# A two-block transformer kernel: maxima from one product over 128 rows, row copies two slots behind TensorE, and the up projections' high and low activations in one product of 512 columns

## The reference

```
m_inter = b + m;  m_t = max(m_inter, max_s d_log)           # running maxima of the mLSTM
w_intra = exp(d_log - m_t);  s = (q k^T) * w_intra          # 8 heads, forward and backward
...
y = concat(m_lat, d_lat) @ w_out
x = x + ga1 * rmsnorm(y, g_post_mix)
h = modulate(rmsnorm(x, g_pre_ffn), sh2, sc2)
u = dwconv3(h @ w_up, conv_w, conv_b)                       # w_up: 2048 x 11264
gate, val = split(u)
x = x + ga2 * rmsnorm((silu(gate) * val) @ w_down, g_post_ffn)
```

## Time and profile before

| | |
|---|---|
| median of 3 runs | 3097.32 us (3096.26 to 3098.8) |
| the profiled execution | 3095.88 us, its span 3093.8 us |
| TensorE busy | 2956.6 us, 96% |
| VectorE, ScalarE, GpSimd busy | 2098.6, 1498.0, 143.8 us |
| mean granted clock | 0.983 |
| HBM | 203 GB/s over the span |

### The profile page before, as it was taken

One profiled execution on the slowest core, in us unless ns is written; L12 is line 12 of the kernel. 1 busy time (PEld: TensorE's weight loads), 2 busy tenths in 40 slices (PEclk: granted clock), 3 DMA queues, 4 the chain that ended last, 5 costly groups with the idle time before them and its releaser, 6 DMA issues.

```text
span 3093.8 us, 44809 instructions
## 1 busy us (share of the span) xinstructions
PE 2956.6 (96%) x17608; PEld 2555.2 (83%) x17608; DVE 2098.6 (68%) x2514; ACT 1498.0 (48%) x1935; POOL 143.8 (5%) x109
## 2 busy tenths in 40 slices
PE   7799999998799999999999889999999999999998
PEld 2478888985679989998997768999987888888876
DVE  6888766557465654665566898754555555899987
ACT  6722222446455544453444423744444444777775
POOL 0000000000000000000000466000000000000000
PEclk9899999999999999999999989999999999999999
DMA  9768777530155555555554334455545655999996
GB/s 373 254 219 297 272 262 244 184 117 28 48 171 163 177 190 190 179 187 190 184 183 150 123 109 150 154 183 188 177 144 164 187 179 176 310 343 347 340 349 240
DMA packets 425402, 628.70 MB, mean 203 GB/s; under 512 B 13168, under 2 KB 234368, under 8 KB 424864
## 3 DMA queue, kind: packets, MB, share of 16 engines
q1 hardware_dynamic: 423504, 615.57, 60.1%
q0 software_dynamic: 1744, 10.98, 0.9%
HBM read 624.40 MB, written 2.10 MB: 203 GB/s over the span
## 4 chain that ended last, share of the span: by engine, by line
PE 86%; DVE 9%; issue 2%; ACT 2%; DMA 1%; POOL 1%; SPq 0%; DVEq 0%; ACTq 0%; POOLq 0%
PE acc L2422 12%; PE acc L2380 11%; PE acc L2419 11%; PE acc L2420 11%; PE acc L2381 11%; PE acc L2383 11%; PE acc L2400 2%; PE acc L2401 2%; PE acc L2403 2%; DVE w_lo L386 1%; DVE w_lo L383 1%; PE acc L2808 1%; PE acc L2806 1%; PE acc L2805 1%; PE acc L2875 1%
## 5 line engine op out<-in xcount | busy, mean ns | idle before, releaser
L368 ACT ACTIVATE w_hi<-w_raw 128x1024 fp32r<-128x1024 f32 x521 | 552.0, 1059 | 771.4 <-PE acc L2383 286.6
L383 DVE TENSOR_TENSOR w_lo<-w_raw,w_hi 128x1024 fp32r<-128x1024 f32 x521 | 641.2, 1231 | 385.7 <-ACT w_hi L368 382.7
L386 DVE TENSOR_TENSOR w_lo<-w_raw,w_hi 128x1024 fp32r<-128x1024 f32 x521 | 649.7, 1247 | 353.3 <-ACT w_hi L370 350.7
L370 ACT ACTIVATE w_hi<-w_raw 128x1024 fp32r<-128x1024 f32 x521 | 549.7, 1055 | 536.8 <-PE acc L2383 303.9
L2380 PE MATMUL acc<-h_pair,w_hi 128*128 128x256 f32 x2368 | 592.8, 287 | 14.6 <-ACT w_hi L368 10.4
L2381 PE MATMUL acc<-h_pair,w_hi 128*128 128x256 f32 x2368 | 589.2, 286 | 0.0
L2380 PEld LDWEIGHTS acc<-h_pair,w_hi 128*128 128x128 f32 x2368 | 461.3, 195 | 23.7 <-issue 23.6
L2381 PEld LDWEIGHTS acc<-h_pair,w_hi 128*128 128x128 f32 x2368 | 461.6, 195 | 0.2
L2419 PE MATMUL acc<-w_hi,h_pair 128*128 128x512 f32 x896 | 354.6, 396 | 14.6 <-ACT w_hi L368 14.3
L2383 PE MATMUL acc<-h_pair,w_lo 128*128 128x256 f32 x2368 | 335.5, 285 | 19.9 <-DVE w_lo L383 19.9
L2420 PE MATMUL acc<-w_hi,h_pair 128*128 128x512 f32 x896 | 350.6, 391 | 0.0
(11 more groups left out here) (501 smaller groups left out, 3663.8 us busy)
## 6 DMA issues: line engine op xcount, KB each, us to landing
w_raw<-in_w_in SPq DMA_DIRECT2D x116, 1024.0 KB, 5.2
w_raw<-in_w_mod SPq DMA_DIRECT2D x96, 1024.0 KB, 5.4
w_raw<-in_w_up SPq DMA_DIRECT2D x176, 512.0 KB, 4.3
w_raw<-in_w_e_gate SPq DMA_DIRECT2D x128, 512.0 KB, 6.0
w_raw<-in_w_e_up SPq DMA_DIRECT2D x128, 512.0 KB, 7.1
w_raw<-in_w_e_down SPq DMA_DIRECT2D x64, 1024.0 KB, 6.7
w_raw<-in_w_down SPq DMA_DIRECT2D x44, 1024.0 KB, 5.0
w_raw<-in_w_out SPq DMA_DIRECT2D x32, 1024.0 KB, 5.1
```

The lines of the kernel that those rows point to most:

```text
L368: act.activation(WHI[:, par, HALVES[0]], RAW[:, r, HALVES[0]], ACT.Copy).then_inc(hi_first, 1)
L370: act.activation(WHI[:, par, HALVES[1]], RAW[:, r, HALVES[1]], ACT.Copy).then_inc(hi_done, 1)
L383: dve.tensor_tensor(WLO[:, par, h0], RAW[:, r, h0], WHI[:, par, h0].bitcast(F32), ALU.subtract)\
L386: dve.tensor_tensor(WLO[:, par, h1], RAW[:, r, h1], WHI[:, par, h1].bitcast(F32), ALU.subtract)\
```

## The change

Three edits.

*Maxima.* The high rows (partitions 0 to 7) and the low rows (32 to 39, put there by a transfer on GpSimd's queue) stand in one tile of 128 partitions, zero elsewhere. A pick with a one in row h and in row 32 + h takes both in one product; so each head and direction has one product over 128 rows in place of two over 8.

*Row copies.* ScalarE's `row_squares` starts in slot 2 in place of slot 1. TensorE transposes x rows 0 and 1 after slot 0 and rows 2 and 3 after slots 2 and 3, alternating between banks 4, 5 and 6, 7; the scale rows 2 and 3 go to banks 2 and 3.

*Up projections.* A high weight tile is held once, and the high and low activations, which lie side by side, move past it as 512 columns into one bank. A block takes four banks. A new first stage puts the two halves together: ScalarE copies the low half to `UR` (128x1024), VectorE adds the high half from PSUM, and frees the banks. The convolution reads `UR` and is the second stage; so four stages stand where three did. The banks of down move so that up and down alternate.

```diff
+                def s0(g, i, b):
+                    wait_block(act, g, i, b)
+                    act.activation(UR[:, b % 2], pair(g, b)[:, :, 1], ACT.Copy).then_inc(stage_sem["a1"], 1)
...
-                feed(act, to_hi, G[f"up{part}"], stages, last=1)
+                feed(act, to_hi, G[f"up{part}"], stages, last=2)
...
+                def s0(g, i, b):                                     # VectorE
+                    wait_stage(dve, "a1", g, i, b)
+                    dve.tensor_tensor(UR[:, b % 2], pair(g, b)[:, :, 0], UR[:, b % 2], ALU.add)\
+                       .then_inc(stage_sem["free"], 1)
...
+            def pairs_move(g, i, b):
+
+                ps = pair(g, b)
+
+                def run(par, q, half, part):
+                    for k in range(SLOT_K)[HALVES[half]]:
+                        kt = SLOT_K * q + k
+                        end = q == g.slots - 1 and k == SLOT_K - 1
+                        for j in range(4):
+                            w = slice(P * j, P * j + P)
+                            if part == HIGH:
+                                last = pe.matmul(ps[:, j], WHI[:, par, k, w], HPAIR[:, kt], start=q == 0 and k == 0,
+                                                 stop=False)
+                            else:
+                                last = pe.matmul(ps[:, j, 0], WLO[:, par, k, w], HHI[:, kt], start=False, stop=end)
+                    return last
+                return run
...
-                if slot_ == 1:
+                if slot_ == 2:
                     scale_rows(0, 2)
                     scale_rows(0, 3)
-                c = slot_ - 1
+                c = slot_ - 2
...
             def rows_in(c):
-                if c:
-                    pe.wait_ge(sem("xt_in"), c)
+                if c == 1:
+                    pe.wait_ge(sem("srow"), 2)
+                if c >= 2:
+                    pe.wait_ge(sem("xt_in"), c - 1)
...
             def beside_wout(c):
                 if c == 0:
                     scale_rows(0, 2)
                     scale_rows(0, 3)
-                if 1 <= c < 5:
-                    rows_in(c - 1)
+                    rows_in(0)
+                    rows_in(1)
+                if c == 2 or c == 3:
+                    rows_in(c)
+                if c == 3:
+                    pe.wait_ge(sem("srow"), 4)
...
+            pool.wait_ge(sem("rounded"), 1)
+            pool.dma_start(NEGMP[32:32 + HEADS], NEGML[:]).then_inc(sem("low_rows"), 16)
...
-                    one = CSTR[0:HEADS, C_REV + h:C_REV + h + 1].broadcast_to([HEADS, P])
-                    for n, part in enumerate((NEGMH, NEGML)):
-                        pe.matmul(bank(4 + d).rearrange("p (r t) -> p r t", r=2), one,
-                                  part[:, d].unsqueeze(1).broadcast_to([HEADS, 2, T]), start=n == 0, stop=False)
+                        pe.wait_ge(sem("low_rows"), 16)
+                    pe.matmul(bank(4 + d).rearrange("p (r t) -> p r t", r=2), PICK[:, h:h + 1].broadcast_to([P, P]),
+                              NEGMP[:, d].unsqueeze(1).broadcast_to([P, 2, T]), start=True, stop=False)
```

More of the change, by code:

```diff
@@ L107 @@
 FFN_PARTS = [(0, 8), (8, 8), (16, 6)]
-UP = ("a1", "free", "a2", "d2", "a3", "d3")
+UP = ("a1", "free", "c1", "d1", "a2", "d2", "a3", "d3")
 for _i, (_f, _n) in enumerate(FFN_PARTS):
@@ L320, in program @@
         STAT = small("row_stats", [P, 48])
+        PICK = small("head_picks", [P, HEADS], F32R)
         DREC = small("d_reciprocals", [P, 2 * HEADS + 1, 2])
@@ L336, in program @@
         HALVES = [slice(0, SLOT_K // 2), slice(SLOT_K // 2, SLOT_K)]
-        stage_sem = {s: sem("blk_" + s) for s in ("free", "a1", "d1", "a2", "d2", "a3", "d3", "mt")}
+        stage_sem = {s: sem("blk_" + s) for s in ("free", "a1", "c1", "d1", "a2", "d2", "a3", "d3", "mt")}
         dve_st = Steps(None, sem("dve_step"))
@@ L476, in last_stages @@
             if c == 2:
-                for f in stages[1:]:
+                for f in stages[2:]:
                     f(g, 0, g.blocks - 1)
@@ L503, in halves_of, with pair @@
             return PS[:, par * 1024:par * 1024 + NB * nw].rearrange("p (w n) -> p w n", w=nw)
+        def pair(g, b):
+            par = (b + int(g.name[2])) % 2
+            return PS[:, par * 2048:par * 2048 + 2048].rearrange("p (j v t) -> p j v t", j=4, v=2)
         def rows_of(g, b):
+            if g.name[:4] == "down":
+                at_ = (4 * (int(g.name[4]) % 2) + 2 * (b % 2)) * NB
+                return PS[:, at_:at_ + TT * NB].rearrange("p (w n) -> p w n", w=TT)
             if g.name != "out2":
@@ L527, in scale_bank @@
         def scale_bank(n, c):
-            return bank(c - 2 if n and c >= 2 else 6 + c % 2)
+            return bank(c - 2 * n if c >= 2 else 6 + c % 2)
         def bank(n, m=NB):
@@ L902, in rows_in @@
                 for u in range(TT):
-                    last = act.activation(XT[:, c, u], bank(4 + u), ACT.Copy)
+                    last = act.activation(XT[:, c, u], bank(4 + 2 * (c % 2) + u), ACT.Copy)
                 last.then_inc(sem("xt_in"), 1)
@@ L1017, in up_stages @@
                 f0 = FFN_PARTS[part][0]
+                def s0(g, i, b):
+                    wait_block(act, g, i, b)
+                    act.activation(UR[:, b % 2], pair(g, b)[:, :, 1], ACT.Copy).then_inc(stage_sem["a1"], 1)
                 def s1(g, i, b):
-                    wait_block(act, g, i, b)
-                    ps, par = narrow(g.b0 + b), b % 2
+                    wait_stage(act, "free", g, i, b)
+                    par = b % 2
                     for j in range(4):
@@ L1039, in s3 @@
                        .then_inc(stage_sem["a3"], 1)
-                return [s1, s2, s3]
+                return [s0, s1, s2, s3]
             for part in range(3):
@@ L1748, in s1 @@
                             st(last)
-                    last.then_inc(stage_sem["free"], 1)
+                    last.then_inc(stage_sem["d1"], 1)
                 def s2(g, i, b):
@@ L1762, in s3 @@
                        .then_inc(stage_sem["d3"], 1)
-                return [s1, s2, s3]
+                return [s0, s1, s2, s3]
             def add_y(g, i, b):
                 wait_block(dve, g, i, b)
-                dve.tensor_tensor(YT[:, b], halves_of(g.b0 + b, TT), YT[:, b], ALU.add).then_inc(stage_sem["free"], 1)
+                dve.tensor_tensor(YT[:, b], rows_of(g, b), YT[:, b], ALU.add).then_inc(stage_sem["free"], 1)
             def scale_y(g, i, b):
@@ L1777, in _ @@
                 stages = up_stages(part)
-                feed(dve, to_lo, G[f"up{part}"], stages, st, 2, last=1)
+                feed(dve, to_lo, G[f"up{part}"], stages, st, 2, last=2)
                 if part == 1:
@@ L2673, in scale_rows @@
                 if n == 0 and c >= 2:
-                    pe.wait_ge(sem("srow"), c - 1)
+                    pe.wait_ge(sem("mixd_done"), 1)
                 if n and c == 2:
@@ L2730, in _ @@
                 if part:
-                    blocks(G[f"up{part}"], here)
+                    blocks(G[f"up{part}"], pairs_move)
                 else:
-                    blocks(G["up0"], here, lambda c: turn(0, c + 2) if c < 2 else None, ready=by_chunk(APPLY["ffn"]), head=2)
+                    blocks(G["up0"], pairs_move, lambda c: turn(0, c + 2) if c < 2 else None, ready=by_chunk(APPLY["ffn"]), head=2)
                 blocks(G[f"down{part}"], inner_rows, ready=by_block(G[f"up{part}"]))
```

33 lines of the change are left out of this document (19 added, 14 removed).

## The result

The changed kernel took 3061.97 us in the median of four runs (3056.83 to 3067.16), the kernel before beside it 3098.06 (3096.26 to 3109.21). The ratio is 0.9877 (95% interval 0.9852 to 0.9902), so the change is faster by 1.2%. The forecast was 3059. The profiled execution took 3063.88 us, its span 3062.1, against 3095.88 and 3093.8: 32.0 us less, where the sum said 38.6.

The account below looks back on a forecast made before the run. Bound: TensorE's stream in the up projections, a chain over three engines in the heads. -18.8 + 2.5 - 18.5 - 3.8 = -38.6 us from 3095.88 gives 3057.3, so 3059 as median; range 3050 to 3068 (0.82).

Parts of the forecast that it names:

- forecast of all parts as read: Whole kernel: all four parts save or cost what was computed, 3054 to 3064 us, chance 0.55.
- Start of wout: Wout's slots 0 to 6: early transposes and later copies remove the ScalarE-TensorE loop; 56.7 becomes 38.2 us, 18.5 saved.
- the walk through the queues: Start of wout: conversions for slots 2 to 5 at 801, 807, 812, 819 meet needs of 809, 815, 822, 827.
- Up projections: Up blocks on TensorE: a pair goes from 0.240 to 0.2267 us, 1408 pairs, 18.8 us saved.
- the rival of the spacing: Up projections: lengthened spacing is not saved, a pair costs 0.237 us, the part gives 3.7 us; 3074 us, chance 0.04.
- The split's lead: Up slots with the convolution: VectorE's weight split leads its low products by 5.6 us; at least 4 us stay, cost 0.
- The rival that ends slower: Up blocks: the weight split starves once its lead is overdrawn by over 1.8 us per block; about 3160 us, chance 0.03.
- Down2: Down2's third slot: the longer chain of up2's last block starts it 2.5 us later; bounds +1.5 and +4.2.
- The clock behind the gap: Down2's third slot: its wait brings a slow clock, +1.7 us, 3061 us, chance 0.12.
- The maxima: mLSTM heads: one product fewer per direction; heads 0 to 4 give 3.2 us, 5 and 6 nothing, 7 0.64; 3.8 saved.
- the price: mLSTM heads: the 128-row maximum product was taken at 0.34 us, as the 8-row one, so widening costs 0.
- The better clock: mLSTM heads: the clock stays up in two slow stretches, 3.4 us more go; 3055 us, chance 0.15.

Follow-up runs that it names:

- The experiment with one slot of distance: Changed kernel with ScalarE's row copies starting in slot 1, transposes still early: wout to up0 106.33 us, against 106.35 in the changed kernel.
- only the up projections: Kernel before with the edit of the up projections alone: 3093.89 us, ratio 0.9965 to the kernel before.
- the changed kernel again: Changed kernel, nothing altered, timed again beside its three single edits on one chip: 3065.3 us, ratio 0.9868 to the kernel before.
- the run with groups of 16: Changed kernel with 16 wide products of an up slot first, then 16 narrow, instead of alternating eights: up0 to down2 673.43 us, against 675.17.
- The two experiments: Kernel before with the maxima edit alone: 3095.61 us, a head 5.55 us; changed kernel with two 128-row maximum products: a head 6.02 us.

## Why the prediction was right, and where it was not

The forecast of all parts as read came true. The measured 3061.97 us lies within its own range of 3054 to 3064. That it lies so near has some luck in it: the up projections gave 3.5 us less than their term, and the maxima by their timed run alone (6.5 us for 3.8, in an interval of 2.8 to 10.6) some 2.7 more.

**Start of wout: right.** Forecast 38.2 us from slot 0 to slot 6, measured 38.1; saved 18.6 there and 19.1 in the stage, with 19.2 for the edit alone. The loop was what the walk through the queues said: ScalarE's copy waited for a transposition made in the slot just ahead. Of the 18.6 us the waits are 14.3; the granted clock over the six slots rose from 0.94 to 1.00, which is 0.06 x 56.7 = 3.4 us more, an estimate, so the rest was mostly clock, as forecast. The experiment with one slot of distance adds that the early transposes do it.

**Up projections: right in mechanism, the term mis-sized.** 15.3 us came, not 18.8. The step that failed is 0.2267 us for every wide product, from the rows of mk. There wide products follow wide ones. Here each group of 8 stands behind narrow ones, and its first five are longer. By the spacings a group of 8 pairs takes 1.842 + 0.952 = 2.794 us against 16 x 0.120 + 8 x 0.120 = 2.880, and 176 groups x 0.086 = 15.1 us. This is the rival of the spacing at a quarter of its strength (3.5 us lost of the 15.1 it named): it had spoken of wide products between narrow ones, and I set it aside because mk's products write four banks in turn as well. That answered one half of it only. Of the rule itself (the Trainium skill, TensorE: Matmul & The Clock Gate, Back-to-back issue gap) the trace bears nothing out: by it the up stage would have given 3.7 us, an estimate, and it gave 15.3.

**The split's lead: right.** VectorE had 131.74 us of work in 190, 69% where 15.8 of 22.2 us is 71%, and no product of line 2427 waited for a low part. The rival that ends slower had its condition nowhere.

**Down2: right.** +2.7 us for +2.5. The clock behind the gap was a rival at 0.12 and +1.7 us. It did not come in the first profile, but it did in two of the six profiles with this gap, only the up projections and the changed kernel again, and there it cost 3.1 and 2.8 us (80.55 and 80.34 against 77.50); in the run with groups of 16 it came in part (79.29 us). It was thus priced and rated too low.

**The maxima: the sum near, its steps wrong.** -3.0 for -3.8 in the first pair of profiles. Two errors met, and the clock hid them. First, the price: I took the form over 128 rows as dear as that over 8, 0.34 us, nearest in place and form, and said 6.16 us per head. It was 5.56. The two experiments split the 1.24 us per head: 0.46 for two products less, 0.78 for the form, 0.30 of it in the mask products behind.

Second, the path. Heads 5 and 6 gave nothing, as forecast. Head 5's products wait for VectorE's norm of the first four heads, and from the end of head 3's products to their start it is 11.4 us before (702.64 to 714.00), after (700.25 to 711.61) and in all thirteen profiles. What the maxima of heads 5 and 6 saved, 2 x 1.24 us, is what the wait grew by (0.89 to 3.38). But I let TensorE pace heads 0 to 4, and it paces 2 to 4. In the changed kernel it waits for ScalarE in front of both maximum products of head 1. Head 3's products before, then the two waits and head 3's products after:

```profile
699.35 3.29 PE L2595 MATMUL acc<-m_v,m_probs 128*128 128x129 f32 x28
```
```profile
676.70 0.50 PE L2621 MATMUL acc<-neg_max_parts,head_picks 128*128 128x512 f32 x1 [0.66 <-ACT m_weights L860]
...
678.20 0.50 PE L2621 MATMUL acc<-neg_max_parts,head_picks 128*128 128x512 f32 x1 [0.89 <-ACT m_weights L860]
...
696.96 3.29 PE L2636 MATMUL acc<-m_v,m_probs 128*128 128x129 f32 x28
```

Heads 2 to 4 at 1.24 us are 3.7; measured from the stage's start, head 3's and head 5's products came 3.9 us earlier. (Each of the two profiles has one stretch at the lower clock ahead of them, of 1.6 us; in the changed kernel again, which has none there, head 5 came 5.5 us earlier.) So the forecast's 3.2 us for this part was near by a price half of the true one and two heads too many. The better clock, a rival at 0.15, did not come: over the stage it was 0.97 before and 0.96 after. Head 5's own products ran faster (3.39 in place of 5.03), but the wait for the mixing grew from 2.20 to 3.15 us, and the 8 score products behind it took 2.72 us in place of 1.97. At the first dense head the changed kernel stood 4.2 us ahead. The other 1.2 went in the dense heads, unchanged work at a lower clock. The tables of these stretches (us, busy us of PE, PEclk, DMA), before and after:

```profile
733.45:794.44 60.99, 45.72 (x293) 1.00 0.09 35
```
```profile
730.76:792.93 62.17, 46.99 (x293) 0.97 0.10 35
```

**The rest of the gap.** The profiled executions differ by 32.0 us, the medians by 36.1, and the ratios of three sets of runs say 1.2 to 1.3%, 37 to 41 us. The 3.0 us that the first and the last stage lost in the first profile are within what these stages show over the thirteen profiles (above), and heads to wout takes 121.7 to 123.9 us in the nine profiles whose heads are those of the changed kernel.

## What to carry to other kernels

Take the price of an instruction from a place with the same neighbours, not only with the same form: 8-row products made the 128-row ones behind them slower, and wide products behind narrow ones cost up to 9 ns more than wide ones behind wide ones. When a stage is a chain over engines, find what starts the next engine's part, and count only what is saved ahead of it: here 11.4 us of VectorE follow head 3's products, so what TensorE saved behind them, 2.5 us, became waiting, and at the stage's start ScalarE took most of what two heads saved. A saving in such a stage is sized by several executions, since a stretch at the lower clock moved it by more than a microsecond. And a wait in a hand-written order is best looked for where an engine copies what another makes in the same slot; one slot of distance was enough, worth 19 us.

## What the hardware showed unexpectedly

- A product over 8 rows and 512 columns is spaced 0.32 to 0.34 us, one over 128 rows 0.23. Of heads that differ in this form alone those with 128 rows are 0.78 us faster each. Fewer rows were dearer. At a change between 8 and 128 rows the weight load starts with its own product, between 128-row products one product ahead.
- After a change from 256 to 512 columns the first five products are spaced 233, 236, 228, 233 and 231 ns, then 227. Why five, stays open.
- A single spacing can mislead where the form changes. The first maximum product of a head is followed after 0.42 us (707.18 to 707.60), the second after 0.23. But the first starts only 0.03 us after the last score product, and score products are spaced 0.22: the two together take 0.45 us, the sum of their usual spacings.
- After idleness of 3.15 us the granted clock over 20 us was 1.00 in four profiles and 0.83 in two, and after the 2.5 us of idleness ahead of up0 it fell in three of thirteen. The same program thus differs by about 3 us at the first place and 1.7 at the second (up0 in 189.90 us in place of 188.23).
